# Five weight tiles loaded as sixteen transfers of eight partitions, and the last layer norm in another order

## What is computed

```python
q = (xf @ wq).reshape(t, 8, 2, 128)
scores = jnp.einsum("thpc,hpnc->thpn", q, sub_keys)
...                                   # the 16 best pairs of each head: ec, softmax: gc
u = jnp.take(u_tab, ec, axis=0)
act = jax.nn.gelu(jnp.einsum("cd,chkd->chk", xc, u)) * gc
vv = jnp.take(v_tab, ec, axis=0)
out = jnp.einsum("chk,chkd->cd", act, vv)
...
x = layer_norm(DEEPNORM_ALPHA * x + f, ln2_g[l], ln2_b[l])
# layer_norm: (x - mean) * rsqrt(var + 1e-5) * g + b
```

## Time and profile before

| what | value |
|---|---|
| median of 3 runs | 3700.55 us (3700.16 to 3709.62) |
| the profiled execution | 3703.69 us, its span 3701.6 us |
| instructions | 42832 |
| busy share of the span | PE 93%, DVE 58%, POOL 46%, ACT 36% |
| DMA | 829.43 MB, mean 224 GB/s |
| load of a weight tile, issue to landing, median | 3.5 us |
| TensorE clock | near full speed throughout (9 tenths or more in 39 of 40 slices) |

### The profile page before, as it was taken

One profiled execution on the slowest core, in us unless ns is written; L12 is line 12 of the kernel. 1 busy time (PEld: TensorE's weight loads), 2 busy tenths in 40 slices (PEclk: granted clock), 3 DMA queues, 4 the chain that ended last, 5 costly groups with the idle time before them and its releaser, 6 DMA issues. The chain is left out here.

```text
span 3701.6 us, 42832 instructions
## 1 busy us (share of the span) xinstructions
PE 3431.5 (93%) x14098; PEld 2364.0 (64%) x14098; DVE 2138.0 (58%) x4139; ACT 1325.2 (36%) x2725; POOL 1687.5 (46%) x1088
## 2 busy tenths in 40 slices
PE   8999999999999999999999999999887777877877
PEld 6888876788888888876888876755433333333333
DVE  5645557433335545566333046788877778767664
ACT  3332326443323332245333233443333233223323
POOL 2545532444454555423444542455554544444442
PEclk9999999999999999999999999999999999999899
DMA  6536420133445445300223331399999999999998
GB/s 247 191 115 237 155 103 2 52 97 96 156 155 184 151 171 214 117 29 13 91 93 99 103 98 47 137 405 421 421 421 422 422 422 421 422 422 422 421 422 348
DMA packets 140657, 829.43 MB, mean 224 GB/s; under 512 B 15705, under 2 KB 16865, under 8 KB 64225
## 3 DMA queue, kind: packets, MB, share of 16 engines
q0 software_dynamic: 73728, 536.90, 34.9%
q1 hardware_dynamic: 66784, 290.73, 22.7%
HBM read 825.48 MB, written 2.10 MB: 224 GB/s over the span
## 5 line engine op out<-in xcount | busy, mean ns | idle before, releaser
L282 POOL TENSOR_TENSOR wlo<-wraw,whi 128x1024 fp32r<-128x1024 f32 x344 | 868.7, 2530 | 1103.6 <-ACT whi L278 1103.5
L278 ACT ACTIVATE whi<-wraw 128x1024 fp32r<-128x1024 f32 x344 | 363.5, 1058 | 652.4 <-DMA wraw<-in_wts 383.1
L289 PE MATMUL f_ps<-f_hh,whi 128*128 128x512 f32 x1344 | 522.8, 389 | 0.0
L290 PE MATMUL f_ps<-f_hl,whi 128*128 128x512 f32 x1344 | 522.8, 389 | 0.0
L291 PE MATMUL f_ps<-f_hh,wlo 128*128 128x512 f32 x1344 | 522.8, 389 | 0.0
L598 DVE TENSOR_TENSOR f_a<-f_sg,f_ps 128x512 f32<-128x512 f32 x88 | 60.5, 687 | 509.1 <-PE f_ps L291 492.7
L2389 ACT ACTIVATE g_dotb<-g_dotb 128x4 f32<-128x4 f32 (+2 forms) x164 | 33.5, 204 | 808.9 <-DVE g_dotb L2636 676.5
L2222 POOL DMA_INDIRECT g_own<-in_uv,idx x185 | 216.6, 1171 | 215.3 <-PE g_psF L2342 125.5
L2222 POOL DMA_INDIRECT g_low<-in_uv,idx x151 | 186.2, 1233 | 227.0 <-PE g_psF L2342 180.7
L290 PEld LDWEIGHTS f_ps<-f_hl,whi 128*128 128x128 f32 x1344 | 252.3, 188 | 52.7
L291 PEld LDWEIGHTS f_ps<-f_hh,wlo 128*128 128x128 f32 x1344 | 252.3, 188 | 52.2
(11 more groups left out here) (551 smaller groups left out, 7130.7 us busy)
## 6 DMA issues: line engine op xcount, KB each, us to landing
wraw<-in_wts SPq DMA_DIRECT2D x356, 512.0 KB, 3.5
m_wrow<-in_ada SPq DMA_DIRECT2D x44, 1024.0 KB, 7.2
m_erow<-in_ada SPq DMA_DIRECT2D x28, 1024.0 KB, 5.2
p_wt<-in_wtok SPq DMA_DIRECT2D x2, 3168.0 KB, 10.2
p_wt<-in_w SPq DMA_DIRECT2D x2, 3072.0 KB, 9.5
g_own<-in_uv,idx POOLq DMA_INDIRECT x185
g_low<-in_uv,idx POOLq DMA_INDIRECT x151
xT<-in_xT SPq DMA_DIRECT2D x2, 1024.0 KB, 17.8
```

The lines of the kernel that those rows point to most:

```text
L278: self.nc.scalar.activation(self.T.whi[:, j % 4], self.T.wraw[:, j % 2], ACT.Copy).then_inc(self.M["w_hi"], 1)
L282: self.nc.gpsimd.tensor_tensor(self.T.wlo[:, j % 4], self.T.wraw[:, j % 2], self.T.whi[:, j % 4].bitcast(F32), ALU.subtract).then_inc(self ...
L289: self.nc.tensor.matmul(out, hi, xh, start=first, stop=False)
L290: self.nc.tensor.matmul(out, hi, xl, start=False, stop=False)
```

## The change

From tile 11 on (tiles 11, 12, 13, 14, 15) a weight tile is loaded as 16 transfers of 8 partitions each, all adding to the semaphore that the one transfer added to; ACT's wait in `round` counts them. The norm first subtracts the mean and multiplies by the scale from PSUM, by halves, without waiting for the square root, and then multiplies by the reciprocal root and adds the shift in one pass (`final`) or in one pass per half (`last_final`). ACT's half of the last norm, DVE's product for it and the semaphore `g_row` are gone.

```diff
+LATE, PIECES = AHEAD[-1] + 1, tuple((p, p + 8) for p in range(0, P, 8))
...
             sp.wait_ge(self.M["w_lo"], n + 1)
-            sp.dma_start(self.raw(n), src).then_inc(self.M["w_in"][n % 2], 16)
+            for p0, p1 in PIECES if n >= LATE else ((0, P),):
+                sp.dma_start(self.raw(n)[p0:p1], src[p0:p1]).then_inc(self.M["w_in"][n % 2], 16)
...
-            apart = sum(1 for a in AHEAD if a < n and a % 2 == n % 2)
-            act.wait_ge(self.M["w_in"][n % 2], 16 * (n // 2 - apart) + 16)
+            landed = sum(len(PIECES) if a >= LATE else 1 for a in range(n % 2, n + 1, 2) if a not in AHEAD)
+            act.wait_ge(self.M["w_in"][n % 2], 16 * landed)
...
-                act.wait_ge(M["g_row"], 1)
-                nc.scalar.activation(r[:, S:2 * S], banks[(TT - 1) % 2][1], ACT.Identity, bias=mv[:, 2:3],
-                                     scale=mv[:, 3:4]).then_inc(M["g_row"], 1)
...
                     nc.vector.bn_aggr(mv[:, 0:2], st[:, :, :]).then_inc(M["g_st"], 1)
+                    dve.wait_ge(M["g_st"], t + 1)
+                    for c in range(2):
+                        nc.vector.scalar_tensor_tensor(r[:, c * S:(c + 1) * S], banks[t % 2][c], mv[:, 0:1],
+                                                       lnp[:, 0, c * S:(c + 1) * S], ALU.subtract,
+                                                       ALU.mult).then_inc(M["g_ch"], 1)
+                    dve.wait_ge(M["g_ch"], 2 * t + 2)
+                    dve.sem_inc(M["g_cp"], 1)
                     dve.wait_ge(M["g_rt"], t + 1)
                     link(nc.vector.reciprocal(mv[:, 3:4], mv[:, 2:3]))
-                    for c in range(2):
-                        nc.vector.tensor_scalar(r[:, c * S:(c + 1) * S], banks[t % 2][c], mv[:, 0:1], mv[:, 3:4],
-                                                ALU.subtract, ALU.mult).then_inc(M["g_ch"], 1)
-                    dve.wait_ge(M["g_ch"], 2 * t + 2)
-                    dve.sem_inc(M["g_cp"], 1)
-                    link(nc.vector.tensor_tensor(r, r, lnp[:, 0], ALU.mult))
-                    nc.vector.tensor_tensor(r, r, lnp[:, 1], ALU.add).then_inc(M["g_fin"], 1)
+                    nc.vector.scalar_tensor_tensor(r, r, mv[:, 3:4], lnp[:, 1], ALU.mult,
+                                                   ALU.add).then_inc(M["g_fin"], 1)
...
+                    dve.wait_ge(M["g_st"], TT)
+                    halves = [slice(c * S, (c + 1) * S) for c in range(2)]
+                    for c, h in enumerate(halves):
+                        link.add(nc.vector.scalar_tensor_tensor(r[:, h], banks[t % 2][c], mv[:, 0:1], lnp[:, 0, h],
+                                                                ALU.subtract, ALU.mult))
                     dve.wait_ge(M["g_rt"], t + 1)
                     link(nc.vector.reciprocal(mv[:, 3:4], mv[:, 2:3]))
-                    nc.vector.scalar_tensor_tensor(mv[:, 2:3], mv[:, 0:1], -1.0, mv[:, 3:4], ALU.mult,
-                                                   ALU.mult).then_inc(M["g_row"], 1)
-                    for c in range(2):
-                        half = r[:, c * S:(c + 1) * S]
-                        if c == 0:
-                            link(nc.vector.tensor_scalar(half, banks[t % 2][0], mv[:, 0:1], mv[:, 3:4],
-                                                         ALU.subtract, ALU.mult))
-                        else:
-                            dve.wait_ge(M["g_row"], 2)
-                        link(nc.vector.tensor_tensor(half, half, lnp[:, 0, c * S:(c + 1) * S], ALU.mult))
-                        nc.vector.tensor_tensor(half, half, lnp[:, 1, c * S:(c + 1) * S], ALU.add).then_inc(M["g_fin"], 1)
+                    for h in halves:
+                        nc.vector.scalar_tensor_tensor(r[:, h], r[:, h], mv[:, 3:4], lnp[:, 1, h], ALU.mult,
+                                                       ALU.add).then_inc(M["g_fin"], 1)
```

More of the change, by code:

```diff
@@ L2146, in peer @@
         M = T.sems.take(nc, "peer", S_SEMS + f"w_ahead*3 x_t x_n x_hi x_lo e_keys e_q e_q0 e_s0 e_s1 e_sc e_sv e_top e_ch e_x e_xo x_c x_cp g_uv*{LOW + TOPS + OWN + SPARE} "
-                                "g_dot g_gelu g_w g_diag g_mm g_ln g_wide g_lnp g_al g_ch g_st g_cp g_rt g_fin g_out g_end g_row h_dif h_exp h_pick h_some")
+                                "g_dot g_gelu g_w g_diag g_mm g_ln g_wide g_lnp g_al g_ch g_st g_cp g_rt g_fin g_out g_end h_dif h_exp h_pick h_some")
         W = Queries(nc, T, M, L * LAYER_T + MIX_T)
```

## The result

| | before | after |
|---|---|---|
| median | 3702.09 us (4 runs, 3700.16 to 3709.62) | 3729.42 us (4 runs, 3728.54 to 3730.51) |
| ratio | | 1.0074, 95% interval 1.0063 to 1.0086 |
| profiled execution, span | 3703.69, 3701.6 us | 3730.51, 3728.4 us |

The change makes the kernel 27 us slower, 0.7%. That is outside the forecast's range; it is the fourth rival, between its two prices.

A forecast was written before the change was run, and what follows sets the result against it. It took the gathers' stage as bound by the fullest DMA engine's bytes. Gathers ending 3.7 us later and the last norm 1.0 us sooner gave +2.7 us on the median 3700.55: 3703.3 us, range 3697 to 3718.

The forecast's parts named there:

- the fourth rival: Eight packets of each late piece, written into neighbouring partitions, hold engines up: some 3715 to 3740 us; chance 0.22.
- The stage is bound by the DMA engines' bytes: Expert gathers, 2400 to 3689 us: length is the fullest DMA engine's bytes over 26.3 GB/s.
- A piece uses eight engines: Late tiles' loads: each 8-partition transfer runs on eight of the 16 DMA engines, with eight completions.
- One fixed eight: Late tiles' loads: every piece uses the same eight engines, each carrying 65.5 KB a tile in place of 32.8 KB.
- +6.7 us on the eight: Five late tiles: the eight engines that carry the pieces get 6.2 us more bytes and 0.5 us more completions.
- -6.2 us on the others: Five late tiles: the eight engines without pieces are relieved of 6.2 us of load.
- a long drain: After the last gather: about eight engines stop some 12 us before the last, the share near 0.5 for long.
- the three laggards: End of the gathers: three engines finish at about 3684.3, 3686 and 3689 us; last relieved, second last loaded, +3.7 us.
- the first rival: End of the gathers: the last engine is among the eight carrying pieces; +5.7 us in all, 3706.3; chance 0.12.
- Latency hidden: Late tiles' loads: landing takes at most 23 plus 3.5 us, covered by 36 us between issue and rounding.
- Norms of tiles 0 to 2 cost and bring nothing: Early norms: one whole-row pass goes, some 1.3 us less three times, worth 0 because DVE idles for DMA.
- The last norm, -1.0 us: Kernel's end: two passes of 0.75 us hide the root; last pass ends 3698.18, 1.0 us sooner.

The follow-up runs named there:

- strided pieces: Changed kernel, but each of the sixteen pieces of eight takes every fourth partition instead of eight neighbours; 1.0034 against the kernel before, 12 us.
- twice: The "once" kernel, but SP waits and loads the same eight pieces again into the same place; 1.0011 against the kernel before, 4 us.
- once: Changed kernel, but only partitions 0 to 63 of the five late tiles are loaded, as eight pieces over every fourth partition; 0.9999 against the kernel before.
- shifted pair: Changed kernel with eight every-fourth-partition pieces from partition 0, or from partition 4, the rest in one or two transfers; 1.0023 and 1.0035 against the kernel before.

## Why the prediction was wrong

The step that failed is the price of a piece beside the gathers. The sum took it as 0 and kept 0.15 to 0.47 us a piece for the fourth rival, with a chance of 0.22; the range ended at 3718. It measured 23.1 / 80 = 0.29 us a piece while the pieces run, and 30.3 / 80 = 0.38 with what is lost between and behind them. The mechanism was named, its place (the pieces between 2475 and 2575 us; in fact to 2594) and both bounds held, but it was set aside for a reason that doesn't carry: the one load of 8 partitions has eight packets of 1 KB, once. A burst of that size shows only as 414 for 421 GB/s over 2 us. Scaled by bytes, it already gave 12 us, two fifths of the loss; that should have been in the forecast, not beside it.

Point by point:

- **The stage is bound by the DMA engines' bytes**: right before the change. After it, by the time of their packets, 0.43 us for 8 KB instead of 0.32 in the second tile's window, at the same busy share.
- **A piece uses eight engines**: right, 253 hardware packets in the second tile's window against 144.
- **One fixed eight**: borne out, by inference. The strided pieces left the gathers' packets nearly alone over partitions 0 to 63 and slowed them over 64 to 127, tile after tile, which rotating eights would not do. The Trainium skill's page "DMA: Bandwidth & Descriptors", section "Why a DMA increments its semaphore by 16 and not by 1", as quoted in the prediction, agrees with that.
- **+6.7 us on the eight**: not shown in the changed kernel alone; twice the lower half, 4 us, fits it in part.
- **-6.2 us on the others**: it is worth nothing, and this step was wrong too, as far as the runs tell. The "once" kernel moves no more gathers in its 160 us than the kernel before. Why is argued, not shown: TensorE is busy 156 of 160 us there in the kernel before, and POOL issues a gather only when a slot is free, so that engines that are ahead run dry and have no lead left when the query tiles end. Then the laggards of the drain stay the laggards, and the test that I named, a long drain, was no test: the changed kernel's drain is about as short as before, and the eight seem fixed all the same. Where the three laggards sit, read from chained packets, was not tested. If the last one is on the eight, as in the first rival, "once" and "twice" would come out as they did too.
- **Latency hidden**: right. No idle time stands before ACT's five rounds in its groups after (0.0 us), and the pieces of a tile land in some 15 us.
- **Norms of tiles 0 to 2 cost and bring nothing**: right, by the norm alone.
- **The last norm, -1.0 us**: it measured -1.3 (5.6 for 6.9 us). The two passes of a pair overlap, 1.41 us for both where I took 1.50.

Of the rivals, the fourth is what happened. Its reason, in the terms of the runs, as far as they tell: a gather packet is held up where another engine's packet goes to the same few partitions, and a piece of eight neighbours sends eight packets to few such places at once. The records carry no engine number, so that it is a matter of which engine writes where is inferred, from the strided halves and the shifted pair, not seen. By the page "SBUF — State Buffer" of the Trainium skill, section "Door 1: The DMA port swizzle", a group of four neighbours (with the group 32 further) is one of 16 ports; the strided and shifted kernels agree with it, 410 to 421 GB/s with each engine at its own group and 357 to 363 at its neighbour's, if the engines write as inferred. Why the shifted pieces cost less than those over partitions 64 to 127 (326 to 345 GB/s) stays open.

## What to carry to other kernels

When the DMA engines are the bound, a load of few neighbouring partitions can cost far more than its bytes: here 0.38 us for 32 KB, which are 0.08 us at 421 GB/s. What the loss went with was not the number of transfers but which partitions they write. So leave a tile as one transfer over all 128 partitions, or cut it by columns; both were free here. Read the rate (GB/s) beside the busy share: here a stage lost a quarter to a third of its throughput (306 and 274 GB/s for 421) with its engines 100% busy. A rival with a mechanism and bounds from a row should be in the sum at its lower bound unless something excludes it.

## What the runs showed that was not expected

- A transfer of 64 partitions (64 to 127), on all engines, also slows the gathers: 290 to 330 GB/s in 4 us windows. Half the partitions is not harmless.
- Transfers of 16 neighbours are worse while they last than those of 8: 279 against 318 GB/s over the first tile, but for 8 us instead of 15.
- The packets slow down alike: the gathers' 8 KB packets go from 0.32 to 0.43 us and the pieces' own 4 KB packets from 0.16 to 0.21. The harm falls on the big stream because it has nearly all of the bytes.
- No version here beats the kernel before by more than its measurement tells; the norm's new order alone is the nearest, at 0.9992.
